# Two 1 MB down pieces of a 128-slot expert asked for ahead of the last two up steps of the 64-slot expert before them

## The reference

```python
def moe_swiglu(xn, w_router, w1, w3, w2):
    ...
    logits = (xf @ w_router).astype(jnp.float32)
    vals, idx = lax.top_k(logits, TOP_K)
    gates = jax.nn.softmax(vals, axis=-1)
    combine = jnp.sum(jax.nn.one_hot(idx, N_EXPERTS, dtype=jnp.float32) * gates[..., None], axis=1)
    y = jnp.zeros_like(xf)
    for e in range(N_EXPERTS):
        y = y + combine[:, e:e + 1].astype(xf.dtype) * swiglu(xf, w1[e], w3[e], w2[e])
```

## Time and profile before

| what | us |
|---|---|
| median of 3 runs | 1227.07 (1226.11 to 1228.47) |
| the profiled execution | 1229.17 |
| its span, first to last instruction | 1227.1 |
| PE busy, of the span | 1162.8 (95%) |
| ACT busy | 559.7 (46%) |
| DVE busy | 665.1 (54%) |

### The profile page before, as it was taken

The page is one execution under the profiler, slowest core; times in us unless marked ns, Lnnn a source line. Parts: engine busy times, 40 slices in busy tenths (PEclk is TensorE's granted clock), DMA queues, the critical chain, the costliest instruction groups (busy, mean ns, idle before and its releaser), DMA issues.

```text
span 1227.1 us, 16270 instructions
## 1 busy us (share of the span) xinstructions
PE 1162.8 (95%) x6555; PEld 858.4 (70%) x6555; DVE 665.1 (54%) x736; ACT 559.7 (46%) x638; POOL 49.6 (4%) x93
## 2 busy tenths in 40 slices
PE   5989899999999999899998999999999989999986
PEld 5979778888879886778637748548568368386351
DVE  4866655545455422797507658038476058474053
ACT  4772454344444565476407547036355056263041
POOL 8010000000000121000000000000000000000000
PEclk9999999999999999899999999999999989999998
DMA  9632259655554421298799999999999999998993
GB/s 318 185 105 71 69 183 364 209 191 182 177 170 151 166 71 64 89 360 292 263 416 413 411 414 413 397 412 414 411 398 377 374 412 412 401 412 323 416 409 128
DMA packets 116736, 351.07 MB, mean 286 GB/s; under 512 B 8136, under 2 KB 55280, under 8 KB 116656
## 3 DMA queue, kind: packets, MB, share of 16 engines
q1 hardware_dynamic: 115552, 347.11, 74.3%
q0 software_dynamic: 1104, 2.86, 0.8%
HBM read 348.89 MB, written 1.05 MB: 285 GB/s over the span
## 4 chain that ended last, share of the span: by engine, by line
PE 84%; DMA 6%; DVE 4%; ACT 3%; POOL 2%; issue 1%; POOLq 0%; SPq 0%; DVEq 0%; ACTq 0%
PE ps L571 20%; PE ps L573 19%; PE ps L572 19%; PE ps L1664 8%; PE ps L1685 6%; DMA arena_c<-in_o_moe_w_dram 5%; PE ps L1609 3%; PE ps L1646 2%; DVE all_lo L1842 1%; PE ps L1621 1%; PE ps L1318 1%; POOL level L689 1%; PE ps L1526 1%; ACT all_hi L831 1%; PE ps L1538 1%
## 5 line engine op out<-in xcount | busy, mean ns | idle before, releaser
L1842 DVE TENSOR_TENSOR all_lo<-arena_c,all_hi 128x1408 fp32r<-128x1408 f32 (+1 forms) x120 | 170.7, 1448 | 217.4 <-ACT all_hi L831 217.3
L831 ACT ACTIVATE all_hi<-arena_c 128x1408 fp32r<-128x1408 f32 (+1 forms) x120 | 146.5, 1246 | 246.3 <-DMA arena_c<-in_o_moe_w_dram 199.9
L1842 DVE TENSOR_TENSOR all_lo<-arena_a,all_hi 128x1408 fp32r<-128x1408 f32 (+1 forms) x96 | 138.2, 1471 | 24.7 <-ACT all_hi L831 24.4
L571 PE MATMUL ps<-all_hi,xg_hi 128*128 128x512 f32 (+1 forms) x384 | 144.9, 377 | 2.9 <-ACT u_act L1080 2.9
L573 PE MATMUL ps<-all_hi,xg_lo 128*128 128x512 f32 (+1 forms) x384 | 144.8, 377 | 0.0
L831 ACT ACTIVATE all_hi<-arena_a 128x1408 fp32r<-128x1408 f32 (+1 forms) x96 | 119.2, 1262 | 56.0 <-PE ps L573 35.3
L572 PE MATMUL ps<-all_lo,xg_hi 128*128 128x512 f32 (+1 forms) x384 | 144.4, 376 | 0.0
L571 PE MATMUL ps<-all_hi,x_hi 128*128 128x512 f32 (+1 forms) x336 | 124.2, 370 | 5.1 <-ACT xn L920 2.4
L1835 DVE TENSOR_TENSOR all_lo<-arena_a,all_hi 128x2048 fp32r<-128x2048 f32 x40 | 91.4, 2289 | 58.0 <-ACT all_hi L824 58.0
L573 PE MATMUL ps<-all_hi,x_lo 128*128 128x512 f32 (+1 forms) x336 | 120.8, 360 | 0.0
L572 PE MATMUL ps<-all_lo,x_hi 128*128 128x512 f32 (+1 forms) x336 | 120.7, 359 | 0.0
(11 more groups left out here) (367 smaller groups left out, 1782.2 us busy)
## 6 DMA issues: line engine op xcount, KB each, us to landing
arena_c<-in_o_moe_w_dram SPq DMA_DIRECT2D x136, 704.0 KB, 9.9
arena_a<-in_o_moe_w_dram SPq DMA_DIRECT2D x120, 704.0 KB, 9.8
arena_c<-in_o_moe_w_dram SPq DMA_DIRECT2D x45, 1024.0 KB, 15.3
arena_a<-in_o_moe_w_dram SPq DMA_DIRECT2D x35, 1024.0 KB, 16.1
arena_c<-in_e_ffn_w_dram SPq DMA_DIRECT2D x36, 512.0 KB, 6.9
arena_a<-in_e_ffn_w_dram SPq DMA_DIRECT2D x30, 512.0 KB, 5.1
arena_a<-in_e_w_in_dram SPq DMA_DIRECT2D x24, 512.0 KB, 8.8
arena_a<-in_o_w_qkv_dram SPq DMA_DIRECT2D x12, 512.0 KB, 4.5
```

Of the source, the lines that this page charges most:

```text
L571: pe.matmul(o, a_hi, b_hi, start=first, stop=False)
L831: act.activation(unit(all_hi, st), in_ring(WHERE[v][0] + off, st.size), ACT.Copy).then_inc(hi_done, 1)
L1842: tt(unit(all_lo, st), in_ring(WHERE[v][0] + off, st.size), unit(all_hi, st).bitcast(F32), ALU.subtract).then_inc(lo_done, 1)
```

## The change

The first two down pieces of the big expert's second half, 1 MB each, are now made (and so placed, numbered and asked for) in front of the last two steps, j = 14 and 15, of the 64-slot up phase. The steps themselves stay where they are. As a piece may now be asked for before others that lie behind it, the counts that SP waits for are made to rise from piece to piece. All later pieces have other places in the ring, since those four changed places with these two at each of four hand-overs.

```diff
+    early = {}
+
+    def down_piece(q, half, j):
+        return new_piece("down", q, half, (j, min(2, HB - j)), min(2, HB - j) * D, big(q))
+
-    for kind, n in WORK:
+    for w, (kind, n) in enumerate(WORK):
         q, a = PHASE[n]
         todo = []
         if kind == "up":
             for j in range(2 * DC):
+                if not big(q) and j == 2 * DC - 2 and big(PHASE[WORK[w + 1][1]][0]):
+                    follows = PHASE[WORK[w + 1][1]]
+                    for k in (0, 2):
+                        early[follows, k] = down_piece(*follows, k)
                 part, halves = (j // 2, j % 2), (a,) if big(q) else (0, 1)
                 on = [(new_piece(kind, q, half, part, HALF, big(q)), 0) for half in halves]
                 todo.append(Step(kind, n, q, a, j, part, HALF, big(q), 0, False, on))
...
                 for j in range(HB):
                     if j % 2 == 0:
-                        v = new_piece(kind, q, half, (j, min(2, HB - j)), min(2, HB - j) * D, big(q))
+                        v = early.get(((q, half), j))
+                        if v is None:
+                            v = down_piece(q, half, j)
                     todo.append(Step(kind, n, q, half, len(todo), j, D, big(q), 0, False, [(v, (j % 2) * D)]))
...
             old = PIECES[v - ARRIVE]
-            assert (seen_units > A_MOE + old.last) if old.big else (seen_raws > old.last)
+            if old.big:
+                seen_units = max(seen_units, A_MOE + old.last + 1)
+            else:
+                seen_raws = max(seen_raws, old.last + 1)
+            WHERE[v] = (WHERE[v][0], seen_units, seen_raws)
```

## The result

| | before | changed |
|---|---|---|
| median of 7 runs, us | 1228.47 (1226.11 to 1231.95) | 1239.00 (1235.29 to 1240.21) |
| span of the profiled execution | 1227.1 | 1238.1 |
| PE busy in it | 1162.8 | 1169.0 |

The ratio is 1.0082, with a 95% interval from 1.0067 to 1.0098: slower by some 10 us. The forecast was 1236.2 us, slower, in a range from 1231 to 1240.5.

What follows compares the result with a forecast made beforehand. DMA and PE are both nearly full; at the end of the 64-slot up phase the full DMA queue is late. Landings 5.1 plus clock 4.0 make 9.1 us on 1229.17, 1238.3, or 1236.2 us on the median's footing; range 1231 to 1240.5.

Steps and rivals of the forecast that it cites:

- The queue is full, so the pairs are late by what is put in front: Up steps 14 and 15: pairs land 5.10 us later; PE waits 4 to 6 us before step 14, 19 to 24 in all.
- less than 5 us later: Sign of a wrong prediction: the pairs of up steps 14 and 15 land less than 5 us later than before.
- The landings cost 5.1 us: Late pairs delay the transposes at hand-overs 1 to 4 by 1.94, 1.48, 0.25 and 1.41 us, sum 5.1 us.
- The clock costs 4.0 us: PE idle before step 14 loses its clock at each hand-over: four times 1.0 us, bounds 2.4 and 7.8 us.
- The rival of a longer low clock: Low clock runs on into step 15 and first down steps: 5.1 + 7.8 us, 1240.0 us; chance 0.07.
- The splits leave the path, the silu wait goes: At hand-overs, down splits finish early, saving some 2.5 us; the transposes' present 0.84 us wait for silu and product goes.
- The delay is passed on: Landings before each 64-slot up phase start from PE's own progress, so each hand-over's delay adds to the next.
- The rival by which it would be taken up again: One unbroken DMA stream paces all hand-overs, only the last delay counts: 1.41 + 1.0 us, 1229.5 us; chance 0.07.
- Footing: Whole kernel: the profiled execution's 1229.17 us lies 2.1 us above the runs' median, so 2.1 us come off the forecast.
- The rival by which the pairs would be in time: DMA has room, pairs of steps 14 and 15 aren't delayed, 9.9 us of split waits go: 1217.2 us; chance 0.06.
- that with a costless clock: Landings cost 5.1 us, the clock nothing, as 64-slot steps at either clock fit into the waits: 1232.2 us; chance 0.12.

Runs made afterwards that it cites:

- hand-over 1 alone: The changed kernel with the two down pieces asked for early at hand-over 1 only, old order at the other three; 1232.57 us, 1.0034 of the kernel before.
- filled change: The changed kernel plus small unused matmuls before up step 14 (26 at hand-overs 1 and 3, 20 at 2 and 4); 1235.39 us, 1.0055 of the kernel before.

## Why the prediction was right

- **The queue is full, so the pairs are late by what is put in front.** Right. The waits in front of step 14 are 4.47, 4.13, 5.10 and 4.16 us (worked out: 5.7, 4.2, 5.1 and as the second), 17.9 us in all where 19 to 24 were forecast, and hand-over 1 alone showed that the order is the cause. At the first, the pair came 1.2 us earlier than worked out (646.98 - 2.95 = 644.03 against 645.2). That is 3.9 us later than before, and "less than 5 us later" was to be a sign of being wrong; so by its letter this sign was met at one hand-over of four. In the filled change, whose step 13 starts within 0.02 us of before's, step 15 started at 648.90, against 648.67 worked out and 643.57 before, so there the full delay is seen, and the landings differ from one execution to the next by a microsecond or so. What makes them differ was not tried.
- **The landings cost 5.1 us.** Somewhat too small. With the clock held the cost is 1235.39 - 1229.15 = 6.2 us (5.2 to 8.4 by the interval). The term that is off is hand-over 3, put at 0.25 us: the lag of the filled change grows by 1.98, 1.41, 1.00 and 1.57 us at the four hand-overs, against 1.94, 1.48, 0.25 and 1.41 worked out. It was read against a profiled execution of before in which hand-over 3 had 6.1 us at half rate and took 12.52 us from step 15 to the transposes (999.36 - 986.84). The kernel with hand-over 1 alone, which does the same there, took 11.26 us (it started step 15 at 990.71), with the clock at 1.00. With the 1.5 us of the neighbours in its place the sum is 6.3 us.
- **The clock costs 4.0 us.** 3.6 us measured, and step 14 ran at half rate at all four hand-overs, as forecast. How the cost splits between landings and clock is less sure than the sum: in the profile of the change the stretch from step 14 to the down phase takes 7.76 us at hand-over 1, 6.57, 7.60 and 7.75 at the others, against 5.92 with the clock held (651.42 - 645.50), so in that execution the clock takes some 6 us and the landings correspondingly less of the 8.1. No run settles this. The rival of a longer low clock had 7.8 us for the term, above both.
- **The splits leave the path, the silu wait goes.** Right: no wait for `all_lo` at a hand-over is left, and the transposes wait for nothing.
- **The delay is passed on.** Right, by the lags of 5.29, 7.02, 8.01 and 11.05 us and by the kernel with hand-over 1 alone, whose lag keeps 3.61 of 3.90 us to the next hand-over. The rival by which it would be taken up again falls.
- **Footing.** 2.1 us were taken off for the profiled execution's distance from the median. Of the 7 runs now known the median is 1228.47, so 1.4 us of the 2.8 us between forecast and result are there; the sum itself was 9.1 us against 9.8 to 10.5 measured. What remains is mostly the hand-over 3 of above. The forecast was right in its mechanism; that each term also came out within some 1 us of the timed runs is in part luck, since it stood on one profiled execution with more half-rate time than usual.

The rival by which the pairs would be in time falls with the 17.9 us of waits; that with a costless clock falls with the filled change.

## What to carry to other kernels

Where a DMA queue is kept full, as here at 408 to 416 GB/s, asking for a piece earlier takes the time from the pieces behind it; ask who waits for those before moving it. Cut the first pieces of the next phase smaller instead, so that the first work on them can start sooner (4 us here), and see that nothing that is ready stands in an engine's program behind work that waits for a later landing (5 us more here). Before a small sum is made against one profiled execution, look for half-rate stretches in the very places that are compared, and take them out of the reading.

## What the runs showed of the hardware

- The same waits cost 3.6 us more with PE idle than with PE kept at work on matmuls of no use: 1238.99 against 1235.39 us. In the first, the up step behind the wait ran at 1.2 GHz (4.96 us for its twelve records), in the second at 2.4 GHz (2.58 us).
- Taking away half-rate time, 47 against 23 us on average, gave back 3.6 us, and not the 12 us that half of the difference would be. So it has to be priced where it lies, and part of it here lay on waits (step 15 of the filled change still waits 0.82 us for its pair).
- Idle times of 2.3 us on PE were followed by a lost clock at hand-overs 2 and 4 of one profiled execution (0.52, 0.64), not at its hand-over 1 (1.00), and at none of three in that of the kernel with hand-over 1 alone (1.00). Filling them gained nothing on average (1.0006).
- Two 704 KB pieces landed within 3.46 us and one of 1024 KB within 2.55 us, at 408 to 416 GB/s, in the old order and in the new one.
